# Two transformer blocks on one core: when the weight slots are refilled around a norm, the order of the norms' steps, and the first loads

## The reference

```
h = h + 0.5 * swiglu(rmsnorm(h, ffn1_norm), gate, up, down)       # "ffn1", width 2816
h = h + mixer(rmsnorm(h, mix_norm))                                # "mix1": three mixers, gated, projected
h = h + 0.5 * swiglu(rmsnorm(h, ffn2_norm), gate, up, down)       # "ffn2"
```

```
x = x + 0.5 * rms_norm(swiglu_2(rms_norm(x, ln_ffn1_pre), ...), ln_ffn1_post)    # "ffn1_2"
x = x + rms_norm(token_mixing(rms_norm(x, ln_mix_pre), ...), ln_mix_post)        # "mix2"
x = x + 0.5 * rms_norm(swiglu_2(rms_norm(x, ln_ffn2_pre), ...), ln_ffn2_post)    # "ffn2_2"
gate = sigmoid(rms_norm(x, ln_ple_pre) @ w_ple_gate)                              # "ple"
x = x + rms_norm(gate * (p @ w_ple_proj), ln_ple_post)
```

## Time and profile before

| | before |
|---|---|
| median of three runs | 2636.69 us (2636.37 to 2637.12) |
| profiled execution, its own time | 2638.0 us |
| its span | 2636.7 us |
| TensorE busy | 2426.3 us, 92% of the span |
| TensorE weight loads busy | 2048.5 us, 78% |
| VectorE busy | 1521.5 us, 58% |
| ScalarE busy | 1246.5 us, 47% |
| GpSimd busy | 50.8 us, 2% |
| moved | 400.12 MB, mean 152 GB/s |
| mean granted clock of TensorE | 0.958 of full speed |
| chain that ended last, by engine | PE 80%, DVE 12%, ACT 6%, issue 2% |

### The profile page before, as it was taken

How to read it: one execution, slowest core, us unless ns; L and a number is a source line. 1 busy time by engine, 2 the same in 40 slices (tenths; PEclk the granted TensorE clock), 3 DMA queues, 4 the chain that set the end, 5 groups by cost and what they waited for, 6 DMA issues and landing times.

```text
span 2636.7 us, 33960 instructions
## 1 busy us (share of the span) xinstructions
PE 2426.3 (92%) x13760; PEld 2048.5 (78%) x13760; DVE 1521.5 (58%) x2356; ACT 1246.5 (47%) x2095; POOL 50.8 (2%) x66
## 2 busy tenths in 40 slices
PE   7998799999999889999999978899988996989996
PEld 6888688788788878878878867678866886867885
DVE  4656576555655657655555565755555547466555
ACT  4445345544544535454454453544445444355444
POOL 0000000000000000000000000000000000000000
PEclk9999899999999989999999989899999998979998
DMA  6554234566565424456555532146544552214552
GB/s 239 187 187 140 79 123 143 169 189 191 173 188 185 142 77 128 141 171 186 190 163 188 186 105 86 57 137 191 187 144 168 190 177 87 92 48 162 189 187 96
DMA packets 110172, 400.12 MB, mean 152 GB/s; under 512 B 12224, under 2 KB 12480, under 8 KB 109632
## 3 DMA queue, kind: packets, MB, share of 16 engines
q1 hardware_dynamic: 110016, 397.96, 46.7%
HBM read 396.86 MB, written 1.05 MB: 151 GB/s over the span
## 4 chain that ended last, share of the span: by engine, by line
PE 80%; DVE 12%; ACT 6%; issue 2%; DMA 0%; POOL 0%; SPq 0%; ACTq 0%; DVEq 0%
PE ps L274 71%; DVE wlo L266 4%; ACT whi L259 3%; PE ps L546 2%; PE ps L1707 1%; DVE alo L406 1%; PE ps L367 1%; ACT ahi L383 1%; PE ps L1156 1%; DVE sm L1204 0%; DMA posi<-pos 0%; DVE cv L2257 0%; ACT nsq L392 0%; PE ps L1121 0%; PE ps L1112 0%
## 5 line engine op out<-in xcount | busy, mean ns | idle before, releaser
L266 DVE TENSOR_TENSOR wlo<-raw,whi 128x1024 fp32r<-128x1024 f32 (+1 forms) x748 | 904.9, 1213 | 708.6 <-ACT whi L259 705.2
L259 ACT CAST whi<-raw 128x1024 fp32r<-128x1024 f32 (+1 forms) x748 | 773.8, 1040 | 663.0 <-PE ps L274 659.4
L274 PE MATMUL ps<-whi,ahi 128*128 128x512 f32 (+2 forms) x1632 | 656.6, 402 | 46.5 <-DVE alo L406 40.5
L274 PE MATMUL ps<-whi,alo 128*128 128x512 f32 (+2 forms) x1632 | 640.4, 392 | 0.0
L274 PE MATMUL ps<-wlo,ahi 128*128 128x512 f32 (+2 forms) x1632 | 638.9, 391 | 0.0
L274 PEld LDWEIGHTS ps<-whi,ahi 128*128 128x128 f32 x1632 | 312.7, 192 | 111.2 <-issue 41.2
L274 PEld LDWEIGHTS ps<-whi,alo 128*128 128x128 f32 x1632 | 311.5, 191 | 63.8
L274 PEld LDWEIGHTS ps<-wlo,ahi 128*128 128x128 f32 x1632 | 313.2, 192 | 58.7 <-issue 0.8
L274 PE MATMUL ps<-whi,yhi 128*128 128x512 f32 (+1 forms) x852 | 336.4, 395 | 2.5 <-DVE ylo L756 1.1
L274 PE MATMUL ps<-whi,ylo 128*128 128x512 f32 (+1 forms) x852 | 332.7, 391 | 0.0
L274 PE MATMUL ps<-wlo,yhi 128*128 128x512 f32 (+1 forms) x852 | 332.6, 390 | 0.0
(11 more groups left out here) (362 smaller groups left out, 2210.1 us busy)
## 6 DMA issues: line engine op xcount, KB each, us to landing
raw<-stream SPq DMA_DIRECT2D x718, 512.0 KB, 3.5
raw<-stream SPq DMA_DIRECT2D x16, 388.0 KB, 3.0
bcb<-bcs SPq DMA_DIRECT2D x9, 512.0 KB, 5.4
raw<-stream SPq DMA_DIRECT2D x8, 416.0 KB, 3.0
raw<-stream SPq DMA_DIRECT2D x4, 384.0 KB, 3.4
cst<-consts SPq DMA_DIRECT2D x1, 1328.0 KB, 7.5
msc<-misc SPq DMA_DIRECT2D x1, 1160.0 KB, 12.7
xs<-xin SPq DMA_DIRECT2D x1, 1024.0 KB, 4.8
```

Source lines behind the costliest of these rows:

```text
L259: act.do.copy(whi[:, n % NSP, 0:w], raw[:, n % NRAW, 0:w]).then_inc(*rounded(n))
L266: dve.do.tensor_tensor(wlo[:, n % NSP, 0:w], raw[:, n % NRAW, 0:w], whi[:, n % NSP, 0:w].bitcast(F), ALU.subtract).then_inc(*rest(n))
L274: m = pe.do.matmul(o, a, b, start=(first and q == 0), stop=(last and q == n - 1))
```

## The change

- `again` in `pe_last`: the beat at which a held piece's slot counts as free is not earlier than `first_time(s + 1) + 1.36 k - 2.6`, where `first_time` is the planned first product of the next stage. So n0 to n3 are placed later in the queues of ScalarE and VectorE. What they wait for is unchanged.
- `dve_post`: the result is first multiplied by the gains alone (one operation per half, behind that half's square and ahead of the power), and behind the power stand two operations, which scale and add in one. `act_post` writes its squares to `nsq` instead of `ptmp`.
- Beats of the plan: `START` of mix2 9.8 instead of 11.1 and of ple 1.4 instead of 2.0; `start_ffn` 0.8 instead of 1.8 behind a `POST` stage; `x_ready` earlier behind `final` and `POST` stages; `turn_time` 2.9 instead of 3.4 behind `x_ready` for mix stages, and 1.0 instead of 0.3 for the last half in the others; `dve_norm` 1.9 instead of 1.6 behind the transposes.
- Feed-forward stages: six slots for activations instead of four; down products 2q - 3 and 2q - 2 follow step q, and those from 17 on follow step 10; the last transposes at beat 2.2 instead of 1.4; `pe_last` one down product later.
- First loads: tile 0 of the stream, the first 136 columns of the constants, the vectors, tile 1, then weights. The rest of the constants goes out at beat 30, `misc` and positions at 75, the first gains at 60 instead of -1. TensorE, ScalarE and VectorE wait for the positions only ahead of mix1 (`tables_in`); the rope tables are computed at beat 100 instead of 60. The first stage waits for each tile of the stream on its own.
- The last store is issued in four halves instead of two tiles.

```
-        return 1.8 if PARTS[s - 1][0] in POST else 0.3
+        return 0.8 if PARTS[s - 1][0] in POST else 0.3
@@ x_ready
-            return end_tile(s, i, 1) + 5.4
+            return end_tile(s, i, 1) + 3.8 + 0.7 * hf
-            return end_tile(s, i, 1) + 3.2 + 1.4 * hf + (1.0 if PARTS[s - 1][0] == "ple" else 0.0)
+            return end_tile(s, i, 1) + 2.6 + 0.7 * hf + (1.2 if PARTS[s - 1][0] == "ple" else 0.0)
@@ turn_time
-        return x_ready(s, i, 1) + 3.4 + 0.5 * hf if scaled(s) else x_ready(s, i, hf) + 0.3
+        if scaled(s):
+            return x_ready(s, i, 1) + 2.9 + 0.5 * hf
+        return x_ready(s, i, hf) + (1.0 if i and hf else 0.3)
+
+    def first_time(s):
+        if s == len(PARTS):
+            return end_tile(s)
+        if PARTS[s][0] == "final":
+            return first_time(s + 1)
+        return end_tile(s) + (start_ffn(s) if PARTS[s][0].startswith("ffn") else START[PARTS[s][0]])
@@ pe_last
+        def again(k, t):
+            return max(t, first_time(s + 1) + 1.36 * k - 2.6)
-                    freed(held[k][0], t + 0.68 * (h + k + 1), dense, s, "held", k)
+                    freed(held[k][0], again(k, t + 0.68 * (h + k + 1)), dense, s, "held", k)
-        freed(held[h - 1][0], t + 1.36 * h, dense, s, "end", 1, 1)
+        freed(held[h - 1][0], again(h - 1, t + 1.36 * h), dense, s, "end", 1, 1)
@@ pe_ffn
-            for j in (2 * q - 2, 2 * q - 1):
-                if j < NFF - h:
-                    yield t + GU * (4 + j % 2)
-                    down(j, t + GU * (4 + j % 2))
-        t = step_beat(s, 10) + 4 * GU + GU * (4 - h) + 0.45
+            for j in (2 * q - 3, 2 * q - 2) if q < 10 else range(17, NFF - h):
+                if j >= 0:
+                    yield t + GU * (5 - j % 2)
+                    down(j, t + GU * (5 - j % 2))
+        t = step_beat(s, 10) + 4 * GU + GU * (5 - h) + 0.45
@@ dve_post
-            yield end_tile(s + 1, i) + 0.9 + late(s)
-            dve.wait_ge(post_act, s, i, 1)
-            dve.do.scalar_tensor_tensor(v, a, 4 * EPS if half else EPS, ...)      # var
-            yield end_tile(s + 1, i) + 2.0 + late(s)
-            dve.wait_ge(post_pool, s, i)
-            for hf in range(2):
-                dve.do.scalar_tensor_tensor(ptmp[:, i, h], source(i, hf), r, bcb[:, h], ALU.mult, ALU.mult)
-            for hf in range(2):
-                dve.do.tensor_tensor(xs[:, i, h], xs[:, i, h], ptmp[:, i, h], ALU.add)
+            for hf in range(2):
+                yield end_tile(s + 1, i, hf) + 0.8 + late(s)
+                dve.wait_ge(post_act, s, i, hf)
+                if hf:
+                    dve.do.scalar_tensor_tensor(v, a, 4 * EPS if half else EPS, ...)
+                dve.do.tensor_tensor(ptmp[:, i, h], source(i, hf), bcb[:, h], ALU.mult)
+            yield end_tile(s + 1, i) + 1.6 + late(s)
+            dve.wait_ge(post_pool, s, i)
+            for hf in range(2):
+                dve.do.scalar_tensor_tensor(xs[:, i, h], ptmp[:, i, h], r, xs[:, i, h], ALU.mult, ALU.add)
@@ sync_program
-        sp.do.dma_start(xs[:, :, :], x_in).then_inc(*load_in("x"))
-        sp.do.dma_start(cst[:, :], consts).then_inc(*load_in("consts"))
+        sp.do.dma_start(xs[:, 0, :], x_in[:, 0, :]).then_inc(*load_x[0](0))
+        sp.do.dma_start(cst[:, 0:near], consts[:, 0:near]).then_inc(*load_in("consts"))
         sp.do.dma_start(vec[:, :], vecs).then_inc(*load_in("vec"))
...
+            yield -3.0
+            sp.do.dma_start(xs[:, 1, :], x_in[:, 1, :]).then_inc(*load_x[1](0))
...
-            sp.wait_ge(resid, len(stages), i, 1)
-            sp.do.dma_start(out[:, i, :], xs[:, i, :]).then_inc(*store(i))
+            for hf in range(2):
+                sp.wait_ge(resid, len(stages), i, hf)
+                sp.do.dma_start(out[:, i, h], xs[:, i, h]).then_inc(*store(i, hf))
```

More of the change, by code:

```diff
@@ L38, in vec_plan @@
     return at, n
-CONST = (("ident", 128), ("bones", 128), ("causal", 256), ("band", 256), ("far", 256),
-         ("later", 256), ("mhalf", 8), ("sel", 512), ("L16", 64), ("L16T", 64), ("L32", 64), ("L32T", 64),
+CONST = (("ident", 128), ("mhalf", 8), ("bones", 128), ("causal", 256), ("band", 256), ("far", 256),
+         ("later", 256), ("sel", 512), ("L16", 64), ("L16T", 64), ("L32", 64), ("L32T", 64),
          ("L64", 64), ("strict", 64), ("incl", 64), ("reset", 256), ("pinv", 64),
@@ L189, in program @@
     load_w = [signal(f"load_w{i}", 16) for i in range(NRAW)]
+    load_x = [signal(f"load_x{i}", 16) for i in range(2)]
     load_in, load_tab, load_bc, store = (signal(x, 16) for x in ("load_in", "load_tab", "load_bc", "store"))
@@ L281, in program @@
     HELD = {"ffn1": 3, "ffn2": 3, "mix1": 4, "ffn1_2": 4, "ffn2_2": 4, "mix2": 4, "ple": 4}
-    START = {"mix1": 3.3, "mix2": 11.1, "ple": 2.0}
+    START = {"mix1": 3.3, "mix2": 9.8, "ple": 1.4}
     GU = 2.72
@@ L333, in wait_x @@
         if s == 0:
-            unit.wait_ge(load_in, "vec")
+            unit.wait_ge(load_x[i], 0)
         else:
@@ L645, in dve_post @@
         for i in range(2):
-            yield end_tile(s + 1, i) + 0.9 + late(s)
-            dve.wait_ge(post_act, s, i, 1)
             a, v, r = stat[:, 8 + 2 * i:9 + 2 * i], stat[:, 12 + i:13 + i], stat[:, 14 + i:15 + i]
-            dve.do.scalar_tensor_tensor(v, a, 4 * EPS if half else EPS, stat[:, 9 + 2 * i:10 + 2 * i], ALU.add,
-                                        ALU.add).then_inc(*post_dve(s, i, "var"))
-            yield end_tile(s + 1, i) + 2.0 + late(s)
-            dve.wait_ge(post_pool, s, i)
-            dve.wait_ge(load_bc, gain_of.index(s))
             for hf in range(2):
                 h = slice(512 * hf, 512 * hf + 512)
-                dve.do.scalar_tensor_tensor(ptmp[:, i, h], source(i, hf), r, bcb[:, h], ALU.mult,
-                                            ALU.mult).then_inc(*post_dve(s, i, "gain", hf))
+                yield end_tile(s + 1, i, hf) + 0.8 + late(s)
+                dve.wait_ge(post_act, s, i, hf)
+                if hf:
+                    dve.do.scalar_tensor_tensor(v, a, 4 * EPS if half else EPS, stat[:, 9 + 2 * i:10 + 2 * i], ALU.add,
+                                                ALU.add).then_inc(*post_dve(s, i, "var"))
+                dve.wait_ge(load_bc, gain_of.index(s))
+                dve.do.tensor_tensor(ptmp[:, i, h], source(i, hf), bcb[:, h], ALU.mult).then_inc(*post_dve(s, i, "gain", hf))
+            yield end_tile(s + 1, i) + 1.6 + late(s)
+            dve.wait_ge(post_pool, s, i)
             for hf in range(2):
@@ L660, in dve_post @@
                 dve.wait_ge(post_dve, s, i, "gain", hf)
-                dve.do.tensor_tensor(xs[:, i, h], xs[:, i, h], ptmp[:, i, h], ALU.add).then_inc(*resid(s + 1, i, hf))
+                dve.do.scalar_tensor_tensor(xs[:, i, h], ptmp[:, i, h], r, xs[:, i, h], ALU.mult,
+                                            ALU.add).then_inc(*resid(s + 1, i, hf))
     def sp_gains():
         for b, s in enumerate(gain_of):
-            yield end_tile(gain_of[b - 1] + 1) + 20 if b else -1.0
+            yield end_tile(gain_of[b - 1] + 1) + 20 if b else 60.0
             if b:
@@ L2411, in gated, with tables_in @@
         return gs[:, i, 512 * hf:512 * hf + 512]
+    def tables_in(unit, s):
+        yield end_tile(s)
+        unit.wait_ge(load_tab, "pos")
     def tensor_program():
@@ L2501, in sync_program, with stream @@
     def sync_program():
-        sp.do.dma_start(xs[:, :, :], x_in).then_inc(*load_in("x"))
-        sp.do.dma_start(cst[:, :], consts).then_inc(*load_in("consts"))
+        near = cat["mhalf"][0] + cat["mhalf"][1]
+        sp.do.dma_start(xs[:, 0, :], x_in[:, 0, :]).then_inc(*load_x[0](0))
+        sp.do.dma_start(cst[:, 0:near], consts[:, 0:near]).then_inc(*load_in("consts"))
         sp.do.dma_start(vec[:, :], vecs).then_inc(*load_in("vec"))
+        def stream():
+            yield -3.0
+            sp.do.dma_start(xs[:, 1, :], x_in[:, 1, :]).then_inc(*load_x[1](0))
         def tables():
-            yield -1.5
+            yield 30.0
+            sp.do.dma_start(cst[:, near:], consts[:, near:]).then_inc(*load_tab("consts"))
+            yield 45.0
             sp.do.dma_start(msc[:, :], misc).then_inc(*load_tab("misc"))
             sp.do.dma_start(posi[:, :], pos).then_inc(*load_tab("pos"))
-        sp.run(by_beat(sp_weights(), tables(), sp_gains()))
+        sp.run(by_beat(sp_weights(), stream(), tables(), sp_gains()))
         for i in range(2):
-            sp.wait_ge(resid, len(stages), i, 1)
-            sp.do.dma_start(out[:, i, :], xs[:, i, :]).then_inc(*store(i))
-        sp.wait_ge(store, 1)
+            for hf in range(2):
+                h = slice(512 * hf, 512 * hf + 512)
+                sp.wait_ge(resid, len(stages), i, hf)
+                sp.do.dma_start(out[:, i, h], xs[:, i, h]).then_inc(*store(i, hf))
+        sp.wait_ge(store, 1, 1)
     tensor_program()
```

31 lines of the change are left out of this document (15 added, 16 removed).

## The result

| | before | after |
|---|---|---|
| median | 2636.9 us | 2603.83 us (2601.44 to 2605.03, 4 runs) |
| ratio, 95% interval | | 0.9873 [0.9856, 0.9890] |
| profiled execution, its span (first to last instruction) | 2638.0, 2636.7 | 2605.03, 2603.4 |
| TensorE busy | 2426.3 | 2420.7 |
| TensorE idle (span less busy) | 210.4 | 182.7 |

The change takes 33.1 us off the median; the forecast was 30.7 (2606, range 2594 to 2621). The two profiled executions differ by 33.3 us of span: 27.7 are idle time of TensorE and 5.6 are busy time, though both run the same 13760 matmuls. The second part goes with the granted clock, 0.958 before and 0.961 after, which the forecast priced only behind a few gaps. Each figure of idle or busy time in this document comes from one profiled execution.

A forecast was written before the change was run, and what follows sets the result against it. Feed-forward stages keep TensorE full; its waits at stage boundaries, the start and the end were taken as the gain. Terms sum to 31.1 us: 2638.0 becomes 2606.9, less 1.3 for the median 2605.6, said as 2606, range 2594 to 2621.

The forecast's parts named there:

- start: Kernel start: smaller first loads bring the first product 5.3 us earlier, less 1.4 for low clock: 3.9 us gained.
- ends of the feed-forward stages: Four stages holding four pieces: a down product fills each 1.5 us wait for `hid`, nothing replacing it: 6.0 us gained.
- ffn to mix1: Two boundaries: n2 precedes the second scale, so the second transposes wait some 1.3 us; a loss of 1.0 each.
- mix1 to ffn: Two boundaries: the last add stands behind fewer casts and product 1 precedes the transposes; 2.4 us each, 4.8 gained.
- through final: One boundary: both scalings precede the casts and `alo` ends at 1341.7 instead of 1342.6; 0.9 us gained.
- ffn_2 to mix2: Two boundaries: earlier stream and transposes, 2 us given back before the first product; 2.7 us each, 5.4 gained.
- ple to ffn_2: One boundary: `alo` stands behind two casts instead of four, tile 1's scale takes some back; 2.9 us gained.
- end: Kernel end: fewer VectorE operations around the last power, so the last store goes earlier; 2.2 us gained.
- pieces of 512 KB: Start, splitting x: at some 250 GB/s five pieces come 4 us later, the start gives nothing and the sum is 27.
- Rival (a): Boundaries: casts become the bound; 2618 if boundaries give a third of their 19.0 us, 2625 if nothing; chance 0.19.
- (b): Raw weight buffers reload later; next pieces one landing late, 3.5 us at each of 13 boundaries, give 2651; chance 0.04.
- (d): Whole kernel: the change does nothing, since beats only order queues; chance 0.01.

The follow-up runs named there:

- u_tail: The changed kernel with the feed-forward ends put back (order of down products, four activation slots, tail's beats): 2608.17 us.
- h_behind: The changed kernel with refill distances chosen per kind of boundary, to put `alo` ahead of casts not yet needed; old beats at two kinds: 2597.38 us.
- r_only: The kernel before the change with only the late refills added: 2622.22 us.
- u_refill: The changed kernel with the refills put back at their old beats, everything else kept: 2614.67 us.
- w_start: The changed kernel with 30 unread transposes of the identity added in TensorE's gap before its first product: 2601.34 us.
- h_post: The changed kernel with late refills only behind stages with a gain, old refill beats behind the others: 2600.56 us.

## Why the prediction was right, by its steps

Measured as the shift of the same work between the two profiles; a step holds what happens inside the mixer beside it:

| step | predicted | measured |
|---|---|---|
| start | 3.9 | 2.0 |
| ends of the feed-forward stages | 6.0 | 7.2 |
| ffn to mix1, two | -2.0 | -2.1 (-2.5, +0.4) |
| mix1 to ffn, two | 4.8 | 4.6 (1.4, 3.2) |
| ffn2 to ffn1 | 1.4 | 1.3 |
| through final | 0.9 | 0.3 |
| ffn_2 to mix2, two | 5.4 | 10.2 |
| mix2 to ffn_2, two | 2.2 | 2.6 |
| ffn_2 to ple, two | 3.4 | 3.7 |
| ple to ffn_2 | 2.9 | 2.0 |
| end | 2.2 | 1.7 |
| sum | 31.1 | 33.5 |

(The spans differ by 33.3; the rest is rounding.)

- **Start**: mis-sized twice. The weights land at 9.07, not 7.5 (the forecast priced the loads that it left out at the old rate), and `alo` stands behind all four `wlo` until 16.06, where I had it end at 15.6; the first product comes at 17.33 and not at 15.7. Then 1.7 us of low clock, where I took 1.4. The later loads of the tables cost nothing that a run shows. The aside on pieces of 512 KB has a sum that is off: at the 363 GB/s that it names, five pieces at 250 come 3.3 us later, not 4. The trace does speak against 250: the kernel before moved 428 GB/s from 9.0 to 14.1 us, in such pieces.
- **Ends**: four times 1.5, and four times 0.3 in the stages that hold three, which I had not counted. That nothing takes its place is false in part (u_tail).
- **ffn to mix1**: cast ahead of `alo`, gap 4.85 where 4.5 was forecast: that part of the mechanism is there, and h_behind shows it. What was priced is not: the second transposes were to wait 1.3 us for the scale, and no such wait stands in the trace. Of the first one's 2.5 us 0.3 are the longer gap, 1.2 low clock behind it, and most of the rest a gap inside the mixer; the second loses 0.3 at the boundary and gains inside. The price agreed with the forecast by luck.
- **mix1 to ffn**: product 1 ahead of the transposes, as forecast, with waits for `wlo` of 0.33 and 0.67. The boundaries give 2.9 and 3.2 us, more than the 2.4 each; the first one's 1.5 us of low clock among the 239 matmuls ahead brings the sum down to the forecast, by luck again.
- **final**: the scalings stand ahead and the old wait for the stream is gone, but `alo` behind the cast ends later by nearly as much.
- **ffn_2 to mix2**: the largest miss, 4.8 us. The transposes came as worked out (5.6 us sooner for both tiles against 5.2 and 5.0 forecast). I then gave 2 us back, and the records give 2.1: the first product is 3.5 sooner. The rest, 1.6 us each, comes inside mix2 behind the first product, where I had priced nothing. In the first mix2 1.5 of it are the 417 matmuls shown above, at a granted clock of 1.00 for 0.95: low clock and not the order. For the transposes r_only shows the refills as the larger part; for the first product the parts overlap.
- **ple to ffn_2**: 0.9 short. The new order multiplies by the gains first, and `var` stands behind that, so the load of the gains comes onto the path:
```profile
1958.92 0.69 DVE L671 TENSOR_TENSOR ptmp<-gs,bcb 128x512 f32<-128x512 f32 x1 [2.16 <-DMA bcb<-bcs]
```
The kernel before has no wait of VectorE for this load. The square that `var` needs was done at 1957.5, and `var` ran at 1959.5. The forecast named no such wait.
- **The other boundaries and the end**: within 0.5 of their terms; at the end the chain of VectorE is all of it.
- **Rival (a)**, casts as the bound, appears at three kinds of place with its waits (`wlo` 6.5 us in 10, the longest 1.1, under the 2 us named). **(b)**: ScalarE waits for a load of weights behind the start 5.1 us in 3 (2.9 in 2 before), the longest 2.0, and no boundary is one landing late. **(d)** fell with the result.

In sum the mechanism was right: later refills and a shorter chain of VectorE free the boundaries behind a gain. The total is closer than the steps were, because a start that was too large stands against a mix2 step that was too small, and at least 1.5 us of that step are low clock that fell elsewhere. What decided is shown by undoing: refills and VectorE's chain cost 11 us each in the median, 4.8 and 6.6 of them idle time; the remainder goes with a lower mean granted clock of those runs (0.957 to 0.961, after 0.961 and 0.962).

## What to carry to other kernels

A cast or refill in an in-order queue is worth placing by what it stands in front of: not as early as its slot is free, nor by one distance for all boundaries, but behind the operation that TensorE waits for and ahead of its own use. Undo the parts singly and together, for one part alone can look worth 15 us (r_only) or 11 (u_refill). When an operation moves ahead in a chain, ask what it alone waits for: here the gain's load. And when loads at the start are moved, look at the order behind them: on top of the moved loads, which gave 1.5 us, two lines of order gave 6.9.

## What the runs showed of the hardware

- The same 603 or 604 matmuls of a stretch with the same idle time took 90.6 to 96.4 us; 0.8 us of shift upstream was enough.
- At the start of the kernel transposes alone came before a rise of the clock: 0.21 us apart up to 11.4 us, 0.11 from 11.5 on (w_start). The profile's row gives 1.00 for both, so at the start of an execution the pace is the thing to read.
- One kernel's runs differed by 10 us, with a mean granted clock of 0.958 in the longest and 0.966 in the shortest (h_post).
- Behind 8 us of idle time the first twelve matmuls took 5.2 us; with 4.4 of the 8 filled by transposes sixteen fit into the same time.
- Filling the long gaps at the boundaries raised the mean granted clock by 0.005 only.
